# Walking the columns of the gate and up products in interleaved runs, and two pairs of them bank by bank

## The reference, cut to what matters

```
x = x + swiglu(rms_norm(x, norm_g[l, 2]), w_gate_up[l], w_down[l])

def swiglu(h, w_gate_up, w_down):
    gate, up = jnp.split(h @ w_gate_up, 2, axis=-1)     # h: 256 x 2048, w_gate_up: 2048 x 11264
    return (jax.nn.silu(gate) * up) @ w_down            # w_down: 5632 x 2048
```

## Time and profile before

| | |
|---|---|
| two runs | 2337.28 and 2339.51 us, median 2338.4 |
| span of the profiled execution | 2335.9 us; its time outside the span is not given |
| TensorE matmuls busy | 2323.2 us, 99%, 10450 instructions |
| TensorE weight loads busy | 1900.1 us, 81%, 10450 instructions |
| VectorE busy | 1418.6 us, 61% |
| ScalarE busy | 1117.7 us, 48% |
| POOL busy | 493.6 us, 21% |
| granted TensorE clock, mean | 1.000 |
| moved by DMA | 460.92 MB, 197 GB/s in the mean |

### The profile page before, as it was taken

How to read it: one execution, slowest core, us unless ns; L and a number is a source line. 1 busy time by engine, 2 the same in 40 slices (tenths; PEclk the granted TensorE clock), 3 DMA queues, 4 the chain that set the end, 5 groups by cost and what they waited for, 6 DMA issues and landing times.

```text
span 2335.9 us, 26565 instructions
## 1 busy us (share of the span) xinstructions
PE 2323.2 (99%) x10450; PEld 1900.1 (81%) x10450; DVE 1418.6 (61%) x1947; ACT 1117.7 (48%) x1448; POOL 493.6 (21%) x568
## 2 busy tenths in 40 slices
PE   9999999999999999999999999999999999999999
PEld 7777878888888888888888888888888888888887
DVE  5676756654556555555455556669994765466554
ACT  6433646544335544444344444544456644444653
POOL 1010011310101110010000011149987322022100
PEclk9999999999999999999999999999999999999999
DMA  9574536766545766666556666655555666654454
GB/s 341 184 246 150 168 133 237 255 222 198 180 136 199 233 195 213 206 204 209 189 195 210 206 203 214 209 188 180 196 182 180 213 219 216 197 174 153 152 166 140
DMA packets 253084, 460.92 MB, mean 197 GB/s; under 512 B 19694, under 2 KB 39849, under 8 KB 252256
## 3 DMA queue, kind: packets, MB, share of 16 engines
q1 hardware_dynamic: 238288, 432.13, 55.6%
q0 software_dynamic: 14672, 27.11, 4.2%
HBM read 432.44 MB, written 2.10 MB: 186 GB/s over the span
## 4 chain that ended last, share of the span: by engine, by line
PE 96%; DVE 2%; ACT 1%; DMA 1%; issue 0%; SPq 0%; ACTq 0%; DVEq 0%
PE ps L97 95%; PE ps L100 1%; DMA RAW<-in_w_in 1%; ACT WHI L103 1%; DVE WLO L109 1%; SPq L138 0%; DVE Alo L120 0%; DVE ED L109 0%; DMA B<-T 0%; ACT WIN L103 0%; ACT BB L103 0%; ACT L103 0%; ACT JUNK L103 0%; ACT Ahi L103 0%; DVE Dlo L120 0%
## 5 line engine op out<-in xcount | busy, mean ns | idle before, releaser
L109 DVE TENSOR_TENSOR WLO<-RAW,WHI 128x1024 fp32r<-128x1024 f32 x701 | 852.0, 1221 | 713.1 <-ACT WHI L103 710.1
L103 ACT ACTIVATE WHI<-RAW 128x1024 fp32r<-128x1024 f32 x793 | 837.1, 1059 | 910.2 <-PE ps L97 903.6
L97 PE MATMUL ps<-WHI,Ahi 128*128 128x512 f32 x1904 | 750.4, 394 | 3.5 <-DVE Alo L120 3.1
L97 PE MATMUL ps<-WHI,Alo 128*128 128x512 f32 x1904 | 740.7, 389 | 0.0
L97 PE MATMUL ps<-WLO,Ahi 128*128 128x512 f32 x1904 | 740.5, 389 | 0.0
L97 PEld LDWEIGHTS ps<-WHI,Ahi 128*128 128x128 f32 x1904 | 357.4, 188 | 85.4 <-issue 7.5
L97 PEld LDWEIGHTS ps<-WLO,Ahi 128*128 128x128 f32 x1904 | 357.5, 188 | 75.0 <-issue 2.4
L97 PEld LDWEIGHTS ps<-WHI,Alo 128*128 128x128 f32 x1904 | 357.4, 188 | 74.8
L109 POOL TENSOR_TENSOR WLO<-RAW,WHI 128x1024 fp32r<-128x1024 f32 x92 | 219.0, 2414 | 52.9 <-ACT WHI L103 52.3
L120 DVE SCALAR_TENSOR_TENSOR ps<-YT,GC,ps 128x256 f32<-128x256 f32 x480 | 188.9, 488 | 8.0 <-ACT ps L103 8.0
L138 POOL DMA_DIRECT2D AC<-TF x88 | 46.5, 536 | 561.8 <-DVE TF L117 558.9
(11 more groups left out here) (318 smaller groups left out, 2218.2 us busy)
## 6 DMA issues: line engine op xcount, KB each, us to landing
RAW<-in_w_gate_up SPq DMA_DIRECT2D x88, 1024.0 KB, 5.1
RAW<-in_a_w_in SPq DMA_DIRECT2D x48, 1024.0 KB, 5.1
RAW<-in_w_down SPq DMA_DIRECT2D x44, 1024.0 KB, 5.0
RAW<-in_w_in SPq DMA_DIRECT2D x39, 1024.0 KB, 6.5
RAW<-in_w_xkv SPq DMA_DIRECT2D x32, 1024.0 KB, 5.6
RAW<-in_w_kv SPq DMA_DIRECT2D x32, 1024.0 KB, 5.8
RAW<-in_b_w_in SPq DMA_DIRECT2D x32, 1024.0 KB, 5.6
RAW<-in_w_out SPq DMA_DIRECT2D x16, 1024.0 KB, 5.1
```

Source lines behind the costliest of these rows:

```text
L97: return self.e.matmul(o, l, r, start=start, stop=stop, skip_group_check=True)
L103: return self.e.activation(o, i, func, scale=scale, **kw)
L109: return self.e.tensor_tensor(o, a, b, op)
```

## The change

Gate and up chunks go through a new function. `COLUMNS` gives each pair i a width c. For c of 4 to 64, moving operand and output are both walked in the same new order: the 512 columns are seen as two halves of 256, and c columns of the first half are followed by c of the second. With c of 256 the two halves follow each other, and with 512 the operand is left as it is. For the pairs in `BANKS_IN_TURN`, 4 and 9, the six matmuls of a tile are sorted so that the two PSUM banks alternate; elsewhere their order is the present one.

```diff
+    COLUMNS = (512, 4, 16, 32, 512, 256, 512, 4, 16, 64, 8)
+    BANKS_IN_TURN = (4, 9)
...
+        def columns_by(c, ap):
+            return ap if c == 512 else ap.rearrange("p (s n c) -> p n s c", s=2, c=c) if c < 256 else \
+                ap.rearrange("p (s c) -> p s c", s=2)
+
+        def ordered_tile(i, ps, ahi, alo, hi, lo, first, last):
+            c = COLUMNS[i]
+            hi, lo, out = columns_by(c, hi), columns_by(c, lo), [columns_by(c, b) for b in ps]
+            terms = [(t, a[:, t * P:(t + 1) * P], w, n) for t in range(2) for n, (a, w) in enumerate(((ahi, hi), (ahi, lo), (alo, hi)))]
+            if i in BANKS_IN_TURN:
+                terms.sort(key=lambda x: x[3])
+            for t, a, w, n in terms:
+                m = e.matmul(out[t], a, w, first and n == 0, last and n == 2)
+            return m
...
                     ahi, alo = (EHI[:, kk - 8, :], ELO[:, kk - 8, :]) if early else (xhi[:, kk, :], xlo[:, kk, :])
+                    if name[0] in ("gate", "up"):
+                        i = ordered_tile(name[1], ps, ahi, alo, hi[:, j, :], lo[:, j, :], k + j == 0, k + j == kt - 1)
+                        continue
                     for t in range(2):
```

## The result

The changed kernel took 2357.47 us in the median of two runs (2356.65 and 2358.29), against 2338.4: a ratio of 1.0083, 95% interval 1.0066 to 1.0099. So it is slower by 19 us. It lies inside the range, but the forecast of no change was wrong.

What follows compares the result with a forecast made beforehand. TensorE's matmuls, busy 99% of the span, were taken as the bound. Banks, reads, writes and others at 0 each, on a 2335.9 us span plus 2.5 us around it, gave 2338.4 us; range 2330 to 2375.

Steps and rivals of the forecast that it cites:

- The bound: Whole kernel: TensorE matmuls busy 99% of the span; any gate or up matmul cost goes one to one into the end.
- Banks in turn: Pairs 4 and 9, 384 matmuls alternating PSUM banks: claimed to cost 0, from eight matmuls of the first half.
- Rival 4: Pairs 4 and 9: alternating banks drop the clock to 1.2 GHz, 77 us more, 2415 us; chance 0.02.
- Writing in runs: Interleaved gate and up pairs, PSUM output: claimed to cost 0, from the differential attention mask's two runs of 128 columns.
- Reading in runs: Interleaved gate and up pairs, moving operand: claimed to cost 0, from cross attention's XK, 8 runs of 32 columns.
- The reservation: Cross-attention rows are plain f32 with twice the time per column, so a small cost at each new run could hide.
- The argument for 0: Interleaved pairs stay at 226.7 ns: every run is a multiple of four columns on a boundary of four.
- Rival 1: Interleaved pairs: a small stop at each of 78,336 run boundaries, 34.7 us, 2373 us; chance 0.08, 0.03 above 2%.
- Rival 2: All 1344 interleaved matmuls run at half rate, 428.3 instead of 226.7 ns: 271 us more, 2609 us; chance 0.07.
- rival 3: Pairs 1 and 7: only runs of 4 suffer, 77.4 us more, 2416 us; chance 0.07.
- Rival 5: Interleaved pairs: a gain of up to 17.9 us, giving 2320.5 us; chance 0.02.
- the 13.3 ns: Gate and up matmuls: part of the 226.7 ns spacing beyond 213.3 ns for 512 columns at 2.4 GHz, left unexplained.

Runs made afterwards that it cites:

- writes_only: Kernel before with only the output of gate and up chunks written in runs of 2 to 128, operand read unbroken, no banks in turn: 2337.42 us, one run.
- half_rate: Kernel before with gate and up unchanged, runs of 2 to 32 columns put in the plain f32 matmuls of back and attend_out: 2339.84 us, one run.

## Why the prediction was wrong, point by point

- **The bound** was read rightly: the loss of the pairs, 19.32 us, went one to one into the chain's long piece (19.33 us) and into the time (19.1 us). ScalarE's wait for PE grew as foreseen, from 128.6 to 137.4 us in the first six pairs, and what lies outside that piece did not grow (the span rose by 18.6 us).
- **Banks in turn** at 0: right. Eight matmuls of the first half carried over to 384, and later to a whole kernel. Rival 4 is out, PEclk stayed at 1.00.
- **Writing in runs** at 0: right, and far beyond the row that it rested on, down to runs of 2. The rule of the Trainium skill ("PSUM — Partial Sum Buffer", Specifications (TRN2)), by which any non-contiguous pattern slows matmuls significantly, does not hold for the output of these fp32r matmuls: writes_only stayed at 43.52 us in every pair. That is shown for two stripes 1024 bytes apart.
- **Reading in runs** at 0 is the step that failed. Its words were "I take 0, the value of the nearest row". XK's 8 runs of 32 columns cost under 1 ns; in the gate and up chunks, 16 runs of 32 cost 10 ns a matmul (6.6 at XK's own distance of 512 bytes) and 128 runs of 4 cost 23.3. The reservation that stood beside it, that a column has twice the time there, pointed at the right place, as half_rate showed: the same runs of 4 that lose 23.3 ns in fp32r at the full rate lose none in plain f32 at half of it. So the row was near in shape but of a kind of matmul that does not pay this price. That the time per column decides fits all but the 29 ns of runs of 2; that the type decides was not tested. The term should have been 19.32 us and was 0.
- **The argument for 0**, that groups of four neighbours are never split, is not enough: every run kept to them, and runs of 4 to 32 still cost 10 to 23.3 ns. "SBUF — State Buffer", Specifications (TRN2), of the Trainium skill has 16-byte lines that want at least two hits for full bandwidth. A run of 4 fills such a line, and with its distance the spacing goes from 3 ns under the unbroken one to 51 over it. A run of 2 puts two columns into a line, so by the letter of that rule it too would be free; it costs 113 ns at 1024 bytes and up to 261 at 256. The rule gives neither; at most, if the first access to a line is not counted as a hit, it has the jump from runs of 4 to runs of 2.
- **Rival 1**, a small stop at each new run, had the kind right, a partial loss in every pair with short runs, and the law wrong. It priced pair 1, pair 10 and pair 3 at 11, 5 and 1.4 us; they took 4.49, 3.20 and 1.92. At 1024 bytes 64 more boundaries cost 6.7 ns between runs of 8 and 4, but runs of 32 already carry 10 ns and runs of 64 nothing, so no price per boundary fits.
- **Rival 2** (all broken patterns at 428 ns) and **rival 3** (only runs of 4) are out. **Rival 5**, a gain, did not come with the orders of the change, but the 13.3 ns are indeed not a floor: another order wins 3.3 of them.

What stays open: what makes the price depend on the distance as in the table, whether the price at distances other than 1024 bytes, and the gain of runs of 4 at 64 bytes, belong to the read alone, why that order beats the unbroken one, what puts it into its slower rhythm, and whether plain f32 is spared by its slower columns or by its type. No other engine was taken away in these runs, so a part of other traffic in it is not excluded.

## What to carry to other kernels

When matmuls bound the kernel, take a price for a read pattern only from rows with the same type and the same time per column; a plain f32 row at half the rate did not show what fp32r pays at the full rate. Walk an fp32r moving operand unbroken or in runs of 64 columns and more, begun where they belong (two columns off, runs of 64 take 252 ns), or try a few orders and read the spacing of starts. The order of the PSUM output cost nothing in two stripes; other orders of it are worth a run of their own. Put several variants in one kernel, one per chunk, and time each from its first matmul to the next one's: differences of 0.1% are plain there that whole runs can't tell.

## What the runs showed of the hardware that was not expected

- Output patterns of two stripes in a PSUM bank are free for these fp32r matmuls, down to runs of 2 columns (43.52 us per pair).
- An fp32r matmul that reads and writes its 512 columns in 32 stripes of 16, four columns of each stripe at a time, starts every 223.3 ns, 3.3 ns under the unbroken one. Over the kernel that is worth 0.8 to 1.0%.
- An unbroken read that begins two columns off costs 6.7 ns a matmul, and one column off 6.1.
- Runs of 4 columns, operand and output alike, are dearest at 256 bytes (278 ns), not at the longest jump (250 ns at 1024).
- Runs of 4, 8, 16 and 32 columns cost a plain f32 matmul of half the rate nothing; runs of 2 cost it 29 ns in 428.
